# Moving VectorE work in a fused two-block kernel: rotation and conv taps behind the gated products, a residual sum one tile later, four taps ahead of a weight remainder

## The chip, the cores and the metric

The kernel runs on one core of a Trainium2 chip. Its time is device time in microseconds (us) for one launch. TensorE (PE in the profile) multiplies, VectorE (DVE) does elementwise work, ScalarE (ACT) applies functions and copies, SyncE (SP) issues weight loads and GpSimd (POOL) does a little elementwise work. Each engine works through its own list in order, and waits on counters that the others raise.

## The reference, cut to what matters

512 positions with 1024 channels pass through two blocks. The first has a conformer branch (a gated product, a causal depthwise convolution of 31 taps, layer norm), a state-space branch with a chunked scan ("the scan"), and a gated feed-forward. The second adds 16 meta positions (528 in all) and runs two layers, called layer 0 and layer 1. What the change touches:

```python
# block 1, conformer branch
v = a * sigmoid(g); v = causal_dwconv(v, dw_w, dw_b)          # 31 taps
# block 2, each layer l
a = rmsnorm(h, mix_pre_g[l]); proj = a @ w_in[l]
q = partial_rope(q, cos, sin); k = partial_rope(k, cos, sin)    # "rotation"
u = c_gate * hc; y = dwconv3(u, conv_w[l]); y_conv = b_gate * y # 3 taps on a gated product
y_attn = sliding_window_gqa_sinks(q, k, v, sinks[l])
h = h + rmsnorm(concat(norm(y_attn), norm(y_conv)) @ w_out[l], mix_post_g[l])
a = rmsnorm(h, mlp_pre_g[l])
h = h + rmsnorm(square(relu(a @ w_up[l])) @ w_down[l], mlp_post_g[l])
```

## The kernel before, in words

**Precision and weights.** Channels lie on the 128 partitions, positions on the free axis; there are eight channel tiles (0 to 7). Every product is made of three passes with fp32r parts: high input times high weight (line 635), low input times high weight (L637), high input times low weight (L639). The weights come as a stream of 1 MB units. SP loads a unit into `raw`, ScalarE copies it to `whi` (L1348, L1431), VectorE subtracts to get `wlo` (L2056, `low_at`, `low_next`), and TensorE then runs the unit. ScalarE's copy waits until TensorE has finished the unit that used the slot. All of it is double-buffered.

**The border of the two layers (lines 3009 to 3041).** The last two down-projection units of layer 0 are computed in two halves of 264 positions. `zadd(u, h)` (L3004) adds a half of such a unit to `zres`, after the unit is done; `zsquares` (L2222, through `add_square_half`) adds its square, made by ScalarE (L1436), into `acc2`. `residual_half(..., 0, ...)` (L2224 to L2247) runs for the first half over tiles k = 0 to 7: scale `zres` (L2239), add it to the residual `hres` (L2241), then `low_half(k - 1)` (L2233), which forms the low part `alo` of the tile before and waits for ScalarE's high part `ahi` of that tile (L1446). After that it runs what `beside` names for k. Before the change the work of the second half stands at k = 0 (`second`: sum and square of the last unit but one), k = 2 (`third`: sum of the last unit) and k = 3 (`fourth`: its square added). ScalarE's own list there is: square of the last unit, weight copy of layer 1's second unit (`split_unit`, L1431), `ahi` of tile 3, root of the second half (L1440), `ahi` of tiles 4 to 7. TensorE's list (`first_units`, L845) is: layer 1's first unit on tiles 0, 1, 2, then the matmul that sums the second half's squares (`sum_half`, L842, which waits for `fourth`), then tiles 3 to 7, then the second unit.

**Layer 1's input projection (lines 1131 to 1180 and 2765 to 2822).** Units 0 to 2 give q, k and v. During unit 3 TensorE multiplies q and k by a swap matrix (`swap`, L1152) and VectorE finishes each rotation (`rope(j)`, three operations, L2770 to L2773; j = 4 is the key). `c_gate(j)` (L2779) reads the first tile of unit 3 + j, `gated(j)` (L2785) reads the second, writes `upad` and frees the PSUM banks. The order on VectorE is `rope(2)`, `rope(3)`, `rope(4)`, `gated(0)`. TensorE, when unit 3 is done, transposes v (L1170), waits for the fourth rotation and v before that and for the fifth (`rope_ok` 5, L1172) after it, and starts unit 4, which also waits for the banks that `gated(0)` frees. The change does not touch TensorE's list.

**The attention steps (lines 2876 to 2912).** Ten steps n share units 4 to 8, a step being half a unit (u = 4 + n // 2, m = n % 2). On VectorE a step has a softmax (L2839 to L2850), a weight remainder, `output(n - 1)` (L2857 to L2863), `conv(u - 4)` when m = 0 (three taps and a scale, L2792 to L2797) and `c_gate` (m = 0) or `gated` (m = 1). TensorE turns the probabilities (L1198, waiting for the exponentials and for the output before last), makes scores (L1182), and runs half a unit around the outputs (L1208). In layer 1 the first block of queries is not needed, so the first step with scores is `n0` = 2, and `second` = 3.

**The long convolution beside `ssm_out` (lines 2573 to 2589).** For each of eight units VectorE adds taps (L2319) for the conformer's tiles, multiplies the unit's result by its gate (`gb`, L2581, after ScalarE's copy into `ring`) and forms the remainder of a coming weight unit. `late_tiles` is [4, 6], so `long_taps(late_tiles, w0, w0 + 2, ...)` is four operations.

Of the kernel before, what the change touches and what calls it, by code (L numbers as in the profile page):

```python
# [39 lines left out]
TAPS_GATE = 3  # L40
# [103 lines left out]
def build(nc, xT, metaT, wstream, cols_d, heads_d, const1_d, const2_d, acs_d, outT):  # L144
    ctx = ExitStack()
    with ctx:
# [214 lines left out]
        def early_scores(n0):  # L361

            return (n0, STEPS - 1) if n0 else (STEPS - 1,)
# [5 lines left out]
        def split2(ap):  # L369
            return ap.rearrange("p (a c) -> p a c", a=2)  # L370

        def col(name, k):
            a = COLS[name][0]
            if isinstance(k, int):
                return cols[:, a + k:a + k + 1]
            return cols[:, bass.ds(k + a, 1)]
# [9 lines left out]
        def cut(t, start, n):  # L386
            return t[:, start:start + n] if isinstance(start, int) else t[:, bass.ds(start, n)]
# [28 lines left out]
        def after(eng, counter, value):  # L416
            eng.wait_ge(counter.sem, value + counter.base)
# [1628 lines left out]
        def _(dve):  # L2046
# [15 lines left out]
            def low_next(stage, i, s):  # L2062

                u = 2 * i + (stage.u0 + s + 2)
                if not by_cast(u):
                    low(stage.slot(s), u, u if CAST0 < u <= CAST_END else None)
# [157 lines left out]
            def residual_half(n, g, span, h, hn, hg, beside):  # L2224

                after(dve, n["std"], h + 1)
                v.reciprocal(span.cols(rstd, h), span.cols(std, h))
                drain()

                def low_half(k):  # L2230
                    if hn is not None:
                        after(dve, hn["hi"], h * KD + k + 1)
                        v.scalar_tensor_tensor(span.half(alo, k, h), span.half(hres, k, h), col(hg, k),  # L2233
                                               span.half(ahi, k, h).bitcast(F32), ALU.mult, ALU.subtract
                                               ).then_inc(hn["lo"].sem, 1)

                for k in range(KD):
                    t, r = span.half(zres, k, h), span.half(hres, k, h)
                    v.scalar_tensor_tensor(t, t, col(g, k), span.cols(rstd, h), ALU.mult, ALU.mult)  # L2239
                    drain()  # L2240
                    v.tensor_tensor(r, r, t, ALU.add).then_inc(n["dve"].sem, 1)  # L2241
                    if k:
                        low_half(k - 1)
                    if k in beside:
                        beside[k]()
                low_half(KD - 1)
# [62 lines left out]
            def long_taps(tiles, a, b, start=None):  # L2309

                for w in range(a, b) if start is None else [start + k for k in range(a, b)]:
                    drain()  # L2312
                    for u in tiles:
                        src, acc = cut(vpad, u * VW + w, T), cut(vout, u * T, T)
                        wc = col("conv_w", u * TAPS + w)
                        if isinstance(w, int) and w == 0:
                            v.tensor_scalar(acc, src, wc, col("conv_b", u), ALU.mult, ALU.add)
                        else:
                            v.scalar_tensor_tensor(acc, src, wc, acc, ALU.mult, ALU.add)  # L2319
# [83 lines left out]
            late_tiles = [u for u in range(4, KD, 2)]  # L2403
# [166 lines left out]
            n = (TAPS - TAPS_GATE) // 4  # L2570
            assert 4 * n + TAPS_GATE == TAPS
            stage_s = WORK["ssm_out"]
            for i in range(0, KD // 2):
                for s in range(2):
                    w0, w1 = (n + 1) // 2 * s, n if s else (n + 1) // 2
                    if i + s == 0:
                        low_next(stage_s, 0, 0)
                    long_taps(late_tiles, w0, w0 + 2, n * i + TAPS_GATE)
                    hold(dve, ring_ok, 2 * i + (s + 1), "dve")
                    t = cut(gb, 2 * T * i + s * T, T)  # L2580
                    v.tensor_tensor(t, t, ring[s][:, :], ALU.mult).then_inc(ring_used, 1)  # L2581
                    if 2 * i + s + 1 < KD:
                        low_next(stage_s, i + s, 1 - s)
                    long_taps(late_tiles, w0 + 2, w1, n * i + TAPS_GATE)
                    w = LAST_TAPS + 2 * (2 * i + s)
                    long_taps([KD - 1], w, min(w + 2, TAPS))
                    w = 5 * (GROUPS - 1) + 2 * (2 * i + s)
                    long_taps([2], w, w + 2)
# [146 lines left out]
            for l, y in enumerate(layers):  # L2735
# [29 lines left out]
                def rope(j):  # L2765
                    after(dve, y["swap_ps"], j + 1)
                    raw_t = qraw[:, j * L:(j + 1) * L]
                    dst = qpad[:, j * QPAD + LEAD:(j + 1) * QPAD] if j < 4 else kpad[:, WIN + LEAD:KPAD]
                    drain()
                    v.tensor_tensor(split2(rot[:, 0:L]), split2(sin), wide(far + 2 * (j % 2)), ALU.mult)  # L2770
                    v.tensor_tensor(rot[:, L:2 * L], raw_t, cos, ALU.mult)
                    drain()
                    v.tensor_tensor(dst, rot[:, 0:L], rot[:, L:2 * L], ALU.add).then_inc(y["rope_ok"].sem, 1)  # L2773
# [7 lines left out]
                def gated(j):  # L2781

                    dve.wait_ge(unit_done, stage.u0 + 4 + j)
                    drain()
                    v.tensor_tensor(split2(upad[j % 2][:, 2:2 + L]), wide(near + 2), split2(cgate[j % 2][:, :]), ALU.mult  # L2785
                                    ).then_inc(psum_free[stage.slot((3 + j) % 2)], 1)

                def conv(j):

                    acc, up_ = yconv[:, j * L:(j + 1) * L], upad[j % 2]  # L2790
                    drain()
                    v.tensor_scalar(acc, up_[:, 0:L], col(w2, 3 * j), None, ALU.mult)  # L2792
                    for w in (1, 2):
                        drain()
                        v.scalar_tensor_tensor(acc, up_[:, w:w + L], col(w2, 3 * j + w), acc, ALU.mult, ALU.add)
                    drain()
                    v.tensor_tensor(acc, acc, rstd[:, :], ALU.mult)  # L2797
# [19 lines left out]
                c_gate(0)  # L2817
                rope(2)
                rope(3)
                rope(4)  # L2820
                gated(0)


                sinks = f"sinks_{l}"
# [52 lines left out]
                ahead, second = early_scores(n0), n0 + 1 if n0 else None  # L2877
                for n in range(STEPS):
                    u, m = 4 + n // 2, n % 2
                    if n >= n0 and n not in ahead and n != second:  # L2880
                        softmax(n)
                    if n == 0:
                        low_at(stage.u0 + 5)
                    elif m == 0:
                        low_at(stage.u0 + u + 1)
                    if n + 1 == second:
                        softmax(second)
                        output(n)
                    if n == 1:
                        conv(0)  # L2890
                    if n > n0 and n != second:
                        output(n - 1)
                    if n and m == 0 and u <= 7:
                        conv(u - 4)
                    if n >= n0 + 3 and m:
                        token_scale((n - 3) // 2)
                    if n + 1 == STEPS - 1:
                        softmax(n + 1)
                    if n == STEPS - 1:
                        add_square(y["n_conv"], 2)  # L2900
                    if u >= 7:
                        b_gate(2 * (u - 7) + m)
                    elif m == 0:
                        c_gate(u - 3)
                    else:
                        gated(u - 3)
                    if n0 and n + 1 == n0:
                        softmax(n0)
                    if n == STEPS - 2:
                        add_square(y["n_conv"], 0)  # L2910
                        add_square(y["n_conv"], 1)
# [102 lines left out]
                args = (y["n_mpost"], f"mlp_post_{l}", span)  # L3014
                folds = (nxt, f"mix_pre_{l + 1}")
# [15 lines left out]
                    zsquares(KD - 1, 1)  # L3031

                if nxt:
                    residual_half(*args, 0, *folds, {0: second, 2: third, 3: fourth})
                    low_at(after_.u0 + 1)
                    residual_half(*args, 1, *folds, {})
                else:
                    last_half(*args, 0, {0: second})
                    third()
                    fourth()  # L3040
                    last_half(*args, 1, {})
# [152 lines left out]
```

## Time and profile before

| | before |
|---|---|
| median of three runs | 2207.59 us (2207.06 to 2208.0) |
| profiled execution, its own time | 2209.11 us |
| span in the profile | 2207.3 us |
| TensorE busy | 2166.7 us, 98% |
| VectorE busy | 1419.1 us, 64% |
| ScalarE busy | 965.8 us, 44% |
| GpSimd busy | 59.0 us, 3% |
| DMA | mean 99 GB/s |

Busy TensorE is modelled from pipelined matmuls, so a successor starts before its predecessor's shown end. In a timeline row the first number is the start, the second the length, and a bracket says how long the engine had been idle and what ended that.

### The profile page before, as it was taken

The numbers are of one execution on the slowest core, as the hardware profiler recorded it, in microseconds if no ns is written. First come the engines' busy times: TensorE is split into PE (matmuls) and PEld (weight loads), VectorE is DVE, ScalarE is ACT, GpSimd is POOL, SyncE is SP. The second block draws the span as 40 slices with busy tenths as digits, with TensorE's granted clock in tenths as the row PEclk, the third lists the DMA queues.
The fourth block names the chain that finished last, engine by engine and source line by source line (L and its number), as shares of the span: only waits on it lengthen the run. The fifth ranks groups of instructions, "written<-read, shape, count | busy, mean of one in ns | idle before, by whom it ended". The sixth has DMA issues, their size and how long they took to land.

```text
span 2207.3 us, 31562 instructions
## 1 busy us (share of the span) xinstructions
PE 2166.7 (98%) x12892; PEld 1894.8 (86%) x12892; DVE 1419.1 (64%) x1830; ACT 965.8 (44%) x1401; POOL 59.0 (3%) x58
## 2 busy tenths in 40 slices
PE   9999999999999999999999999999999999999997
PEld 6887777788788888888999999999999989888887
DVE  4876898999868555645876784145367668622544
ACT  5447776632625444423457443133233664422321
POOL 1000111000000000000000000000000000000001
PEclk9999999999999999999999999999999999999999
DMA  4234556222222222243211222222222112222221
GB/s 155 96 110 130 155 160 159 90 96 96 86 103 80 96 96 96 97 153 134 100 58 58 77 83 91 96 91 82 96 77 100 58 60 94 96 96 96 95 96 58
DMA packets 36843, 217.63 MB, mean 99 GB/s; under 512 B 5056, under 2 KB 7104, under 8 KB 12128
## 3 DMA queue, kind: packets, MB, share of 16 engines
q1 hardware_dynamic: 27504, 182.99, 23.8%
q0 software_dynamic: 2880, 20.97, 4.0%
q10 hardware_dynamic: 6320, 11.70, 1.7%
q8 instruction: 101, 1.65, 0.3%
q14 instruction: 38, 0.31, 0.0%
HBM read 213.48 MB, written 2.16 MB: 98 GB/s over the span
## 4 chain that ended last, share of the span: by engine, by line
PE 77%; DVE 12%; ACT 3%; DVEq 3%; issue 2%; DMA 2%; ACTq 1%; POOL 0%; SPq 0%; POOLq 0%
PE PS L635 24%; PE PS L639 24%; PE PS L637 24%; DVE vout L2319 4%; DVE wlo L2056 2%; PE PS L1208 1%; DVEq L2312 1%; DMA wlo<-weights 1%; PE PS L1182 1%; PE PS L1198 1%; ACT m_slot L1606 1%; DVE acc L2211 0%; DVE hres L2241 0%; PE PS L1223 0%; ACTq L1608 0%
## 5 line engine op out<-in xcount | busy, mean ns | idle before, releaser
L639 PE MATMUL PS<-ahi,wlo 128*128 128x512 f32 (+2 forms) x2333 | 704.3, 337 | 0.0
L635 PE MATMUL PS<-ahi,whi 128*128 128x512 f32 (+2 forms) x2237 | 677.6, 340 | 7.4 <-DVE wlo L2056 2.2
L637 PE MATMUL PS<-alo,whi 128*128 128x512 f32 (+2 forms) x2237 | 667.3, 335 | 0.0
L2056 DVE TENSOR_TENSOR wlo<-raw,whi 128x2048 fp32r<-128x2048 f32 x160 | 366.3, 2290 | 427.6 <-ACT whi L1348 426.3
L1348 ACT ACTIVATE whi<-raw 128x2048 fp32r<-128x2048 f32 x156 | 298.8, 1916 | 634.4 <-PE PS L639 631.8
L639 PEld LDWEIGHTS PS<-ahi,wlo 128*128 128x128 f32 x2333 | 404.8, 188 | 46.9
L635 PEld LDWEIGHTS PS<-ahi,whi 128*128 128x128 f32 x2237 | 387.6, 188 | 64.7 <-issue 14.6
L637 PEld LDWEIGHTS PS<-alo,whi 128*128 128x128 f32 x2237 | 386.9, 188 | 42.8 <-issue 1.0
L635 PE MATMUL PS<-f2hi,whi 128*128 128x264 f32 (+2 forms) x800 | 214.9, 314 | 0.0
L637 PE MATMUL PS<-f2lo,whi 128*128 128x264 f32 (+2 forms) x800 | 214.9, 314 | 0.0
L639 PE MATMUL PS<-f2hi,wlo 128*128 128x264 f32 (+2 forms) x800 | 214.8, 314 | 0.0
L2319 DVE SCALAR_TENSOR_TENSOR vout<-vpad,cols,vout 128x512 f32<-128x512 f32 x240 | 178.5, 754 | 18.1 <-issue 1.9
L635 PEld LDWEIGHTS PS<-f2hi,whi 128*128 128x128 f32 x800 | 136.1, 188 | 8.7
L637 PEld LDWEIGHTS PS<-f2lo,whi 128*128 128x128 f32 x800 | 135.9, 188 | 8.9
L639 PEld LDWEIGHTS PS<-f2hi,wlo 128*128 128x128 f32 x800 | 135.8, 189 | 8.8
L1966 ACT ACTIVATE f2hi<-rl 128x528 fp32r<-128x528 f32 (+1 forms) x64 | 40.7, 639 | 112.5 <-DVE rl L2971 112.3
L635 PE MATMUL PS<-fhi,whi 128*128 128x512 f32 x176 | 69.0, 392 | 0.0
L639 PE MATMUL PS<-fhi,wlo 128*128 128x512 f32 x176 | 68.5, 389 | 0.0
L637 PE MATMUL PS<-flo,whi 128*128 128x512 f32 x176 | 68.5, 389 | 0.0
L2070 DVE SCALAR_TENSOR_TENSOR fg<-PS,cols,fg 128x511 f32<-128x511 f32 x88 | 63.8, 745 | 4.3 <-ACT fg L1750 1.0
L1821 ACT ACTIVATE sc<-sc,small 128x256 f32<-128x256 f32 (+1 forms) x72 | 34.9, 486 | 50.3 <-DVEq L2851 50.3
L2975 DVE TENSOR_TENSOR f2lo<-rl,f2hi 128x528 fp32r<-128x528 f32 (+1 forms) x64 | 44.4, 696 | 19.1 <-ACT f2hi L1966 16.2
(389 smaller groups left out, 2823.9 us busy)
## 6 DMA issues: line engine op xcount, KB each, us to landing
raw<-weights SPq DMA_DIRECT2D x169, 1024.0 KB, 4.8
wlo<-weights POOLq DMA_DIRECT2D x10, 1024.0 KB, 9.1
acs_b<-acs_rows ACTq DMA_DIRECT2D x20, 256.0 KB, 5.1
raw_hi<-weights POOLq DMA_DIRECT2D x5, 1024.0 KB, 5.6
whi<-weights POOLq DMA_DIRECT2D x5, 1024.0 KB, 10.3
const<-const ACTq DMA_DIRECT2D x2, 1232.0 KB, 5.3
x_in<-x_t SPq DMA_DIRECT2D x4, 512.0 KB, 6.0
out_t<-hres SPq DMA_DIRECT2D x16, 128.0 KB, 1.7
```

Source lines behind the costliest of these rows:

```text
L635: nc.tensor.matmul(o, wh, h, start=first, stop=False)
L637: nc.tensor.matmul(o, wh, h, start=False, stop=False)
L639: mm = nc.tensor.matmul(out[j], wl, hi[j], start=False, stop=last)
L1182: mm = nc.tensor.matmul(bank(far + z, 256 - k0, jj * 256 + k0), qpad[64 * z:64 * z + 64, j * QPAD + b * WIN:j * QPAD + (b + 1) * WIN], kpa ...
L1198: mm = nc.tensor.transpose(bank(far + 2 + kb, P, j * P), sc[n % 2][:, j * 256 + kb * P:j * 256 + (kb + 1) * P], ident)
L1348: nc.scalar.activation(whi[slot][:, :], raw[slot][:, :], ACT.Copy).then_inc(hi_ready, 1)
L1821: nc.scalar.activation(p, p, ACT.Exp, bias=small[:, 8 * z + j:8 * z + j + 1], accum_out=small[:, 16 + 8 * z + j:17 + 8 * z + j])
L1966: nc.scalar.activation(cut(f2hi, 4 * W * i + (2 * s + m) * W, W), rl[2 * s + m][:, 0:W], ACT.Copy).then_inc(f2hi_ok.sem, 1)
L2056: v.tensor_tensor(wlo[s][:, :], whole[:, :], high[:, :].bitcast(F32), ALU.subtract).then_inc(lo_ready, 1)
L2070: return v.scalar_tensor_tensor(acc[:, sh:n], ps[:, 0:n - sh], w, acc[:, sh:n], ALU.mult, ALU.add)
L2319: v.scalar_tensor_tensor(acc, src, wc, acc, ALU.mult, ALU.add)
L2975: v.tensor_tensor(cut(f2lo, c, W), rl[2 * s + m][:, 0:W], cut(f2hi, c, W).bitcast(F32), ALU.subtract).then_inc(f2lo_ok.sem, 1)
```

## The change

It moves VectorE instructions within VectorE's list in four places; no instruction is added or removed, and no other engine's list changes.

1. In the first pass of the loop beside `ssm_out`, four taps stand ahead of the weight remainder `low_next(stage_s, 0, 0)` instead of behind it.
2. In layer 1, `gated(0)` stands ahead of `rope(4)`; layer 0 keeps its order.
3. In layer 1's step 2, `conv(1)` leaves its place ahead of `c_gate(2)` and stands behind `gated(2)` in step 3. In layer 0 `second` is None and nothing changes.
4. At the border, `third` stands at tile 3 instead of 2 and `fourth` at tile 4 instead of 3.

```diff
@@ the loop beside ssm_out
+                    long_taps(late_tiles, w0, w0 + 2, n * i + TAPS_GATE)
                     if i + s == 0:
                         low_next(stage_s, 0, 0)
-                    long_taps(late_tiles, w0, w0 + 2, n * i + TAPS_GATE)
@@ each layer, before the steps
                 rope(2)
                 rope(3)
+                if l:
+                    gated(0)
                 rope(4)
-                gated(0)
+                if not l:
+                    gated(0)
@@ the steps
-                    if n and m == 0 and u <= 7:
+                    if n and m == 0 and u <= 7 and n + 1 != second:
                         conv(u - 4)
...
                         gated(u - 3)
+                    if n == second:
+                        conv(u - 4)
@@ the layers' border
-                    residual_half(*args, 0, *folds, {0: second, 2: third, 3: fourth})
+                    residual_half(*args, 0, *folds, {0: second, 3: third, 4: fourth})
```

## Rows read from the trace of the kernel before

**Rows 1.** Page, busy us (share of span) and instructions, each engine.
```profile
PE 2166.7 (98%) x12892; PEld 1894.8 (86%) x12892; DVE 1419.1 (64%) x1830; ACT 965.8 (44%) x1401; POOL 59.0 (3%) x58
```
**Rows 2.** Waits of TensorE from 1620 to 1700: total us, times, longest.
```profile
PE PS L635 <- DVE alo L2233: 2.0, 5, 0.6
```
**Rows 3.** Timeline of VectorE, the border: start us, length us, operation [idle before].
```profile
1635.12 0.43 DVE L3004 TENSOR_TENSOR zres<-zres,PS 128x264 f32<-128x264 f32 x1 [1.35 <-PE PS L639]
...
1636.61 0.49 DVE L2233 SCALAR_TENSOR_TENSOR alo<-hres,cols,ahi 128x264 fp32r<-128x264 f32 x1
1637.19 0.43 DVE L2222 TENSOR_TENSOR acc<-acc,sq 128x264 f32<-128x264 f32 x1
...
1638.45 0.49 DVE L2233 SCALAR_TENSOR_TENSOR alo<-hres,cols,ahi 128x264 fp32r<-128x264 f32 x1
...
1639.77 0.49 DVE L2233 SCALAR_TENSOR_TENSOR alo<-hres,cols,ahi 128x264 fp32r<-128x264 f32 x1
```
**Rows 4.** Timeline of ScalarE, the border.
```profile
1635.96 1.90 ACT L1431 ACTIVATE whi<-raw 128x2048 fp32r<-128x2048 f32 x1
1637.77 0.50 ACT L1446 ACTIVATE ahi<-hres,cols 128x264 fp32r<-128x264 f32 x1
1638.64 0.48 ACT L1440 ACTIVATE std<-PS,cols 128x264 f32<-128x264 f32 x1 [0.38 <-PE PS L842]
1639.02 0.51 ACT L1446 ACTIVATE ahi<-hres,cols 128x264 fp32r<-128x264 f32 x1
```
**Rows 5.** Timeline of TensorE, the border.
```profile
1637.15 0.39 PE L635 MATMUL PS<-ahi,whx 128*128 128x264 f32 x1 [0.62 <-DVE alo L2233]
...
1638.00 0.61 PE L842 MATMUL PS<-acc,const 128*128 128x264 f32 x2
...
1645.91 0.36 PE L635 MATMUL PS<-ahi,whi 128*128 128x264 f32 x1 [1.22 <-DVE wlo L2056]
```
**Rows 6.** Timeline of VectorE, layer 1's last rotation and first gated product.
```profile
1691.41 0.70 DVE L2770 TENSOR_TENSOR rot<-const,PS 128x528 f32<-128x528 f32 x1
...
1693.61 0.71 DVE L2785 TENSOR_TENSOR upad<-PS,cgate 128x528 f32<-128x528 f32 x1
```
**Rows 7.** Timeline of ScalarE there: the weight copy released by unit 3's end.
```profile
1693.30 1.92 ACT L1348 ACTIVATE whi<-raw 128x2048 fp32r<-128x2048 f32 x1 [13.88 <-PE PS L639]
```
**Rows 8.** Timeline of TensorE there: the start of unit 4.
```profile
1694.47 0.48 PE L635 MATMUL PS<-ahi,whi 128*128 128x264 f32 x2 [0.66 <-DVE upad L2785]
```
**Rows 9.** Timeline of VectorE, layer 1's steps 2 to 4.
```profile
1721.66 0.49 DVE L2792 TENSOR_SCALAR yconv<-upad,cols 128x528 f32<-128x528 f32 x1
...
1724.71 0.71 DVE L2779 TENSOR_TENSOR cgate<-PS,mu 128x528 f32<-128x528 f32 x1
...
1726.31 1.23 DVE L2839 SCALAR_TENSOR_TENSOR sc<-PS,const 128x1024 f32<-128x1024 f32 x1
...
1732.21 0.42 DVE L2863 TENSOR_TENSOR y_tok<-PS,small 128x256 f32<-128x256 f32 x1
```
**Rows 10.** Timeline of TensorE, the same steps.
```profile
1726.35 0.48 PE L635 MATMUL PS<-ahi,whi 128*128 128x264 f32 x2 [1.08 <-DVE upad L2785]
...
1734.06 1.04 PE L1198 MATMUL PS<-const,sc 128*128 128x128 f32 x8
```
**Rows 11.** Timeline of ScalarE, the copy released by unit 5's end.
```profile
1723.37 1.91 ACT L1348 ACTIVATE whi<-raw 128x2048 fp32r<-128x2048 f32 x1 [0.60 <-PE PS L639]
```
**Rows 12.** Timeline of VectorE, the first pass beside ssm_out.
```profile
470.05 2.29 DVE L2056 TENSOR_TENSOR wlo<-raw,whi 128x2048 fp32r<-128x2048 f32 x1 [2.84 <-ACT whi L1348]
472.43 2.90 DVE L2319 SCALAR_TENSOR_TENSOR vout<-vpad,cols,vout 128x512 f32<-128x512 f32 x4
...
476.18 2.29 DVE L2056 TENSOR_TENSOR wlo<-raw,whi 128x2048 fp32r<-128x2048 f32 x1 [0.24 <-ACT whi L1348]
```
**Rows 13.** Windows: stretch, length, PE, PEld, DVE, ACT, POOL busy, granted clock, DMA.
```profile
14.00:18.00 4.00, 4.00 (x40) 1.64 (x39) 2.19 (x4) 2.52 (x4) 2.37 (x1) 0.57 0.02 4
362.00:372.00 10.00, 7.72 (x42) 6.18 (x42) 9.33 (x18) 6.58 (x11) 0.65 (x1) 1.00 0.77 197
```

## The prediction

> **What bounds the kernel now.** I read the page first: TensorE is busy 2166.7 us of a span of 2207.3 us [rows 1], so only about 40 us are left in which it does nothing, and a reordering on VectorE can act only on those holes or make new ones. Next I asked for TensorE's waits by stretch, then for the timelines of the three engines at each of the four places. What the reader is to see: in the stretch of the border TensorE waits five times for VectorE's low parts, 2.0 us in all [rows 2], and once 1.22 us for a weight remainder [rows 5]; at layer 1's unit 4 it waits 0.66 us and at unit 6 1.08 us for a gated product [rows 8, 10]. These are the holes that the change aims at, 5 us together, or 0.22% of the time.
>
> **The border.** No part of the change adds or removes an instruction or a DMA; each moves some on VectorE, and what SP loads depends on them only through the weight remainders. Take times as before the change until something moves. VectorE waits 1.35 us ahead of `third` for the last unit's end, and `third` starts at 1635.12 [rows 3]. With tile 3's two operations and `alo` of tile 2 ahead of it, this hole is filled: `alo` of tile 2 starts earlier by the hole's 1.35 us and by the 0.58 us that a sum takes with its drain (1637.19 - 1636.61 [rows 3]), at 1634.7, and its 0.49 us end just as `third` may start. So TensorE runs tile 2 with no wait (0.62 us saved [rows 5]) and `third` starts at the same 1635.12. Then tile 4's two operations follow, in the place of tile 3's, to 1636.6. Next in VectorE's list is `alo` of tile 3, and it needs ScalarE's `ahi` of tile 3. ScalarE's list has the 1.90 us weight copy ahead of that, from 1635.96, released by the same unit's end; `ahi` of tile 3 runs from 1637.77 to 1638.27 [rows 4]. Before the change VectorE came for it at 1638.45, after `fourth`; now it comes 1.7 us too early and stands still with `fourth` queued behind it. `alo` of tile 3 starts at 1638.30, `fourth` 0.58 us later (1637.19 - 1636.61 [rows 3]) at 1638.88 and ends at 1639.31. TensorE took 0.85 us for tile 2 (1638.00 - 1637.15 [rows 5]), would be through it at about 1637.3, and waits for `fourth` ahead of L842. L842 moves from 1638.00 to about 1639.38, 1.38 later. ScalarE's root follows L842 by 0.64 us (1638.64 - 1638.00 [rows 4, 5]), so at 1640.02, and `ahi` of tile 4 comes 0.38 behind it at 1640.40 to 1640.91 [rows 4]. `alo` of tile 4 starts at 1640.95 instead of 1639.77 [rows 3]: 1.18 us late. From there the loop is VectorE's chain as before, tile by tile, then the weight remainder for the second unit, for which TensorE was already waiting (1.22 us [rows 5]); so the second unit starts 1.18 us later, at 1647.1, and VectorE and ScalarE are late by the same. Cost: +1.2 us. Bounds: if L842 followed `fourth` with no distance and the other distances shrank by a drain, +0.8; if TensorE is slower to pick up after a hole of 2 us, +1.6. A gain here would need `ahi` of tile 3 early: the hole of 1.35 us that is filled, less 0.04 us of rounding, -1.3. ScalarE's order is untouched, so I take +1.2.
>
> **The last rotation.** VectorE's three rotation operations start at 1691.41 and the gated product behind them at 1693.61 [rows 6], 2.20 us later, of which 0.09 is the drain that shows between any two dependent operations (470.05 + 2.29 to 472.43 [rows 12]). Unit 3 ends when ScalarE's copy is released, 1693.30 [rows 7], so the rotation lies wholly beside TensorE's unit 3: it costs nothing. With the product ahead of it, VectorE waits from 1691.4 to about 1693.38 with the rotation queued behind; the product takes its 0.71 us, to 1694.09, the rotation starts a drain later, at 1694.18, and ends 2.11 us on, at 1696.29. TensorE's unit 4 waits for both. Before, it started 0.15 us after the product's end (1693.61 + 0.71 to 1694.47 [rows 6, 8]); now the rotation is what comes last, and it starts at 1696.44. Cost: +1.97 us, the wait going from 0.66 to 2.63. Behind the rotation on VectorE stands a weight remainder for unit 5, and behind that the load on SP's queue that it releases; TensorE needs the first when unit 4 ends and the second a unit later. Bounds: the rotation's 2.20 us whole, and 1.8 if the product is released 0.2 us sooner than ScalarE's copy shows. A gain is excluded as long as L1172 stands: the later of the two can't come earlier in this order.
>
> **The conv taps.** `conv(1)` takes 3.05 us (1724.71 - 1721.66 [rows 9]). Without it `c_gate(2)` starts at 1721.66, `gated(2)` must wait for unit 5, whose end shows in ScalarE's release at 1723.37 [rows 11], and runs 1723.42 to 1724.13, while TensorE is still busy with turning and scores. The wait of 1.08 us ahead of unit 6 goes [rows 10]. Then `conv(1)` runs from 1724.22 to 1727.2 and the softmax of step 4 starts at 1727.27, where it started at 1726.31 [rows 9]: 0.96 later. Behind it in VectorE's list are a weight remainder and the output that TensorE needs before it turns the next probabilities. That output ends at 1732.63 + 0.96 = 1733.59 [rows 9]; TensorE would come for it at 1734.06 - 1.08 = 1732.98 [rows 10], and with 0.15 us of release it starts at 1733.74. So 0.76 of the 1.08 us is given back there, and 0.32 stays. ScalarE's next steps are 0.96 late as well and cost at most another 0.1 at the turn of the output tile. I take -0.3. Bounds: -1.1 if nothing is given back, +1.0 if the 0.96 us of delay passes to TensorE whole.
>
> **The four taps.** VectorE idles 2.84 us ahead of the remainder at 470.05; four taps take 2.90 and stood right behind it [rows 12]. They fit into the hole to within 0.1 us. But the next remainder, at 476.18, was waiting for ScalarE already (0.24 us [rows 12]), and ScalarE for TensorE. So the hole only moves behind the gate product, and everything from 476.18 on is as before. TensorE has no wait in this stage. 0.0 us; bounds -0.24 and +0.1.
>
> **The sum.** 1.2 + 1.97 - 0.3 + 0.0 = +2.9 us. The profiled execution took 2209.11 us for its span of 2207.3, 1.5 over the median of the runs; it would take 2212.0 and its span 2210.2. Against the median: 2207.59 + 2.9 = 2210.5 us, 0.13% more. About 0.2%, 4.4 us, is what a measurement of this kernel can tell from no change.
>
> **Rivals.** *A, the border is neutral or gains* (2208.6 us): if the wait for `ahi` of tile 3 costs VectorE only what the hole ahead of `third` gave, as two ends of one exchange, the border comes out between -1.3 and +0.6, say -0.7, and 1.97 - 0.3 - 0.7 = +1.0. For it: VectorE is what TensorE waits for here. Against: `fourth` lies behind the wait, and L842 and the root hang on `fourth`. *B, all holes close* (2205.0 us): the gated product, not the rotation, is what releases unit 4, so that its banks come 0.2 us sooner; the conv's whole 1.08 and the border's whole 1.3 are gained: -2.6, 0.12% faster. For it: each hole in the trace names exactly the operation that now comes earlier. Against: L1172, the 1.90 us copy [rows 4], and the output [rows 9]. *C, the clock falls* (2212.2 us or more, slower): TensorE now stands still for about 2.1 us at the border and 2.6 us ahead of unit 4. After a sparse stretch with short matmuls near the start the granted clock of 14 to 18 us is 0.57, so some 3.4 us of the 4 ran at the lower level of 1.2 GHz [rows 13]; where TensorE sets the pace, half of that, 1.7 us, is lost. One such fall gives 2.9 + 1.7 = +4.6, and two +6.3 (2213.9); the first already passes 4.4 us. Against: the stretch 362 to 372 has 2.28 us without TensorE work and a clock of 1.00 [rows 13], and the hole at unit 4 has dense work on both sides. The border is where it would decide, since TensorE would wait there ahead of nearly each tile.
>
> The Trainium skill, "TensorE: Matmul & The Clock Gate", Part 1, says that the clock drops to half after a stretch in which TensorE was idle and comes back only with sustained activity. By that rule a long enough hole would cost as in C; the trace agrees with a fall, and shows with the 2.28 us hole that one of this size alone need not bring it.
>
> **Chances.** Forecast 0.66; A 0.15; B 0.06; C 0.13. The forecast's own range, from its bounds, is 2208.9 to 2212.3. The range for 8 in 10 takes in most of A and the lower case of C: 2207.6 to 2212.4. Faster than 0.2% needs -4.4 us, which not even B gives: 0.02. Slower than 0.2% is C and the forecast's upper edge (rotation 2.2, border 1.6, conv +1.0): 0.13. The rest, 0.85, is within 0.2%.
>
> **What would show it.** In the changed kernel: VectorE's `alo` of tile 3 waits over 1 us for ScalarE's L1446, TensorE waits some 2 us ahead of L842, and the wait for the second unit's `wlo` stays near 1.2. Ahead of unit 4 of layer 1 TensorE waits 2.6 us and the releaser is `kpad` (L2773), not `upad`. The wait of 1.08 us for `upad` is gone and one of 0.6 to 0.8 us stands ahead of L1198, 8 us on. In the first pass beside `ssm_out` the idle of 2.8 us stands ahead of the second remainder instead of the first. I am wrong if unit 4 is released by `upad`, if L842 starts before 1638.5 relative to the same border, or if the granted clock falls in the windows behind either hole.

## The result, and the profile after

The changed kernel takes 2211.62 us in the median of 17 runs (2210.25 to 2216.32); the kernel before, run between them, 2208.32 (2206.6 to 2211.71). The ratio is 1.0020, with an interval of 1.0013 to 1.0026: slower by 2.9 to 5.7 us, clear of no change. The medians are 3.3 us apart and the means 3.8. With the later runs the means are 2212.6 (28 runs) and 2208.6 (118 runs of the kernel before): 4.0 us. The time lies in my range, and the sum's +2.9 us is near it, but I had given 0.85 to "within 0.2%", which I took for what can't be told from no change.

TensorE's waits after the change (waiting instruction, releaser, total us, times, longest), first from 1620 to 1700, the border and the rotation, then from 1730 to 1800, the steps:

```profile
PE PS L635 <- DVE kpad L2773: 2.5, 1, 2.5
PE PS L842 <- DVE acc L2222: 2.1, 1, 2.1
PE PS L635 <- DVE alo L2233: 0.8, 1, 0.8
PE PS L635 <- DVE wlo L2056: 0.8, 1, 0.8
PE PS L1152 <- DVE qpad L2773: 0.3, 1, 0.3
...
PE PS L1198 <- DVE y_tok L2866: 0.7, 1, 0.7
```

Both holes of the forecast are there: 2.1 us ahead of L842, where before L842 waited for nothing [rows 5], and 2.5 us ahead of unit 4 with `kpad` as releaser in place of 0.66 us with `upad` [rows 8]. The 1.08 us ahead of unit 6 [rows 10] are gone and 0.7 us ahead of L1198 have come.

VectorE at the border after the change, to be held against [rows 3]; this execution came to the border 1.31 us sooner, so `third` at 1633.81 answers to 1635.12:

```profile
1633.28 0.49 DVE L2233 SCALAR_TENSOR_TENSOR alo<-hres,cols,ahi 128x264 fp32r<-128x264 f32 x1
1633.81 0.43 DVE L3009 TENSOR_TENSOR zres<-zres,PS 128x264 f32<-128x264 f32 x1
...
1636.98 0.49 DVE L2233 SCALAR_TENSOR_TENSOR alo<-hres,cols,ahi 128x264 fp32r<-128x264 f32 x1 [1.61 <-ACT ahi L1446]
1637.57 0.43 DVE L2222 TENSOR_TENSOR acc<-acc,sq 128x264 f32<-128x264 f32 x1
...
1639.72 0.49 DVE L2233 SCALAR_TENSOR_TENSOR alo<-hres,cols,ahi 128x264 fp32r<-128x264 f32 x1 [0.81 <-ACT ahi L1446]
```

`third` no longer waits. `alo` of tile 3 waits 1.61 us for ScalarE's `ahi`, with the square's sum (L2222) queued behind it. ScalarE's and TensorE's side of the same stretch, with the copy of 1.90 us ahead of that `ahi`:

```profile
1634.65 1.90 ACT L1431 ACTIVATE whi<-raw 128x2048 fp32r<-128x2048 f32 x1
1636.46 0.49 ACT L1446 ACTIVATE ahi<-hres,cols 128x264 fp32r<-128x264 f32 x1
1638.81 0.48 ACT L1440 ACTIVATE std<-PS,cols 128x264 f32<-128x264 f32 x1 [1.86 <-PE PS L842]
```

```profile
1638.06 0.71 PE L842 MATMUL PS<-acc,const 128*128 128x264 f32 x2 [2.11 <-DVE acc L2222]
1640.27 0.39 PE L635 MATMUL PS<-ahi,whx 128*128 128x264 f32 x1 [0.78 <-DVE alo L2233]
1645.87 0.36 PE L635 MATMUL PS<-ahi,whi 128*128 128x264 f32 x1 [0.76 <-DVE wlo L2056]
```

VectorE at the rotation, against [rows 6]: it stands still 2.04 us for the gated product, then rotates. TensorE's unit 4 starts 0.05 us after `kpad` is done:

```profile
1693.27 0.71 DVE L2785 TENSOR_TENSOR upad<-PS,cgate 128x528 f32<-128x528 f32 x1 [2.04 <-PE PS L639]
1694.07 0.70 DVE L2770 TENSOR_TENSOR rot<-const,PS 128x528 f32<-128x528 f32 x1
...
1695.47 0.71 DVE L2773 TENSOR_TENSOR kpad<-rot 128x528 f32<-128x528 f32 x1
```

```profile
1696.23 0.51 PE L635 MATMUL PS<-ahi,whi 128*128 128x264 f32 x2 [2.52 <-DVE kpad L2773]
```

The four taps now fill ScalarE's 2.84 us [rows 12], and the hole has moved to the next remainder, as worked out; TensorE waits nowhere in that stage:

```profile
466.00 2.90 DVE L2319 SCALAR_TENSOR_TENSOR vout<-vpad,cols,vout 128x512 f32<-128x512 f32 x4
468.81 2.28 DVE L2056 TENSOR_TENSOR wlo<-raw,whi 128x2048 fp32r<-128x2048 f32 x1
...
474.86 2.29 DVE L2056 TENSOR_TENSOR wlo<-raw,whi 128x2048 fp32r<-128x2048 f32 x1 [3.16 <-ACT whi L1348]
```

What I had not priced, and had named as a sign that I am wrong, shows in a window behind the border's hole (PE, PEld, DVE, ACT, POOL busy, granted clock, DMA share, GB/s): the clock is 0.57.

```profile
1640.00:1644.00 4.00, 3.73 (x17) 3.54 (x18) 3.67 (x9) 2.13 (x4) 0.00 (x0) 0.57 0.01 2
```

**Stretches.** Whole spans differ by several us from one execution to the next before they even reach the border: the copy L1431 starts between 1632.5 and 1638.2 us in the 14 profiles, and of all edits only that of the taps stands ahead of it. So each edit is read between marks of its own profile. *Border*: from the start of that copy (just behind the last unit's end) to the second unit's first matmul. *Rotation*: from there to unit 4's first matmul. *Steps*: from there to the first matmul of the output projection (L646). What is left behind that is 414.7 to 414.9 us in all. The clock was looked through up to the last matmuls; the tail, in which TensorE is done, is left out of the column.

| kernel | border | rotation | steps | edits in it; where the clock fell (below 0.99 in a 4 us window) |
|---|---|---|---|---|
| before | 9.95 | 48.56 | 98.08 | none; start |
| changed | 11.22 | 50.36 | 98.02 | all; border |
| e1 | 11.22 | 48.52 | 98.00 | rotation undone; border |
| e2 | 9.94 | 50.40 | 97.96 | border undone; scan |
| e3 | 11.52 | 48.32 | 97.99 | late wait; border |
| e4 | 11.97 | 50.37 | 99.42 | border's hole filled; unit 4 |
| e5 | 9.53 | 50.41 | 99.33 | tile 3 early; scan, unit 4 |
| e6 | 9.79 | 50.40 | 98.02 | fourth first; start |
| e7 | 9.94 | 48.55 | 97.96 | conv alone; none |
| e8 | 8.63 | 48.26 | 99.11 | repaired; none |
| e9 | 11.31 | 50.40 | 98.04 | unit 4's hole filled; start, border |
| e10 | 8.63 | 48.30 | 96.99 | conv in step 5; start, scan |
| e11 | 11.23 | 50.42 | 99.52 | all again; start, border, unit 4 |
| e12 | 9.95 | 50.41 | 99.63 | rotation alone; unit 4 |

Against the kernel before, the change costs 1.27 at the border and 1.80 at the rotation and brings 0.06 in the steps: +3.0 us with an undisturbed clock.

### The profile page after: what moved, and what is told of

Same layout as the page of the kernel before. It is cut to its first block, busy times and chain, and to the rows that moved or that the text cites. A ratio compares the mean times of both kernels' runs of the same rounds, so it can differ in the third digit from the quotient of the medians.

```text
span 2209.0 us, 31562 instructions
## 1 busy us (share of the span) xinstructions
PE 2166.7 (98%) x12892; PEld 1896.6 (86%) x12892; DVE 1419.1 (64%) x1830; ACT 965.4 (44%) x1401; POOL 59.0 (3%) x58
## 4 chain that ended last, share of the span: by engine, by line
PE 79%; DVE 12%; ACT 3%; DVEq 3%; issue 2%; DMA 1%; ACTq 1%; POOL 0%; POOLq 0%
PE PS L635 25%; PE PS L639 24%; PE PS L637 24%; DVE vout L2319 4%; DVE wlo L2056 2%; PE PS L1208 1%; DVEq L2312 1%; DMA wlo<-weights 1%; PE PS L1182 1%; PE PS L1198 1%; ACT m_slot L1606 1%; DVE acc L2211 0%; DVE hres L2241 0%; PE PS L1223 0%; ACTq L1608 0%
## 5 line engine op out<-in xcount | busy, mean ns | idle before, releaser
L1348 ACT ACTIVATE whi<-raw 128x2048 fp32r<-128x2048 f32 x156 | 298.8, 1916 | 634.3 <-PE PS L639 631.7
```

The lines of the kernel that those rows point to most:

```text
L1348: nc.scalar.activation(whi[slot][:, :], raw[slot][:, :], ACT.Copy).then_inc(hi_ready, 1)
```

## The experiments

**e1, the rotation undone.** The second hunk of the change taken back.

> The change without its second edit (layer 1 rotates before the gated product again). My theory: the wait of TensorE ahead of unit 4 falls from 2.5 us (released by kpad, L2773) to 0.66 us (released by upad), and the kernel takes 1.85 us less than the changed one: about +1.0 us against the kernel before in the traces (border +1.27, conv -0.3). Rival, the clock: if the hole ahead of unit 4 also lets TensorE's clock fall in some executions, undoing it takes off more than 2 us on average and the spread of the times gets smaller. Rival, the rotation is hidden: less than 0.5 us.

Measured: 2209.4 us (median of 12), ratio 1.0006 (0.9997 to 1.0014). The wait ahead of unit 4 is 0.64 us again, the rotation's stretch 48.52: 1.84 us off, as expected. Its mean is 2209.8, 2.8 us below the changed kernel's, which leans to the clock's part; but the spread of its times is no smaller (6.7 us against 6.1), as that rival had wanted.

**e2, the border undone.** The last hunk taken back.

> The change without its fourth edit (third and fourth at tiles 2 and 3 again). My theory: no wait of 2.1 us ahead of L842, alo of tile 3 waits for nothing, and 1.2 us less than the changed kernel: about +1.6 us against the kernel before (rotation +1.85, conv -0.3). Rival, the clock: the granted clock of 0.57 that the changed kernel shows in the 4 us behind that hole is what makes its slow executions (2213 to 2216 us, clock 0.993 to 0.996); then this kernel has no such fall, its runs lie within 1.5 us of each other as those before, and its mean is over 2 us lower than that of the changed kernel.

Measured: 2210.88 us, ratio 1.0012 (1.0004 to 1.0021). The border's stretch is 9.94, 1.28 off. The mean is 2.5 us over that of the kernel before, where 1.6 was expected, and a run of 2216.54 is among the twelve, so the rival fell in that form: the border's hole is not what makes the slowest executions.

**e3, the wait put where the rotation is needed.**

```diff
-                after(pe, y["rope_ok"], 5)      # ahead of unit 4
...
+                    if n == n0:
+                        after(pe, y["rope_ok"], 5)   # ahead of the first scores
```

> The changed kernel, with TensorE's wait for the fifth rotation moved from ahead of unit 4 to ahead of the first scores (two half units later in layer 1). My theory: the order gated product before rotation costs only through this wait; now unit 4 starts 0.15 us after the gated product, the wait is about 0.4 us and is released by upad, and the kernel takes 2.0 us less than the changed one, 0.9 us over the kernel before. Rival: the gated product itself comes late for another reason (release of unit 3), then the wait stays above 1 us.

Measured: 2208.81 us, ratio 0.9995 (0.9986 to 1.0003). Unit 4 waits 0.41 us and is released by `upad`; the stretch is 48.32, 2.04 off and 0.24 under the kernel before. So the new order at the rotation is good in itself, and L1172 alone turns it into a loss. The whole time missed the expectation: the stretches of this profile add up to +1.2 us against the kernel before, +0.9 was expected, and the mean is 0.4 below it, with an interval that ends at +0.7. Why these runs were so fast is open.

```profile
1694.23 0.48 PE L635 MATMUL PS<-ahi,whi 128*128 128x264 f32 x2 [0.41 <-DVE upad L2786]
```

**e4, the border's hole filled.** `spin(14, ...)` ahead of `sum_half` in `first_units`.

> The changed kernel, with 14 small matmuls (128x128, into the bank of the sum that follows) ahead of L842 at the border, so that TensorE works through most of its hole of 2.1 us. If the fall of the clock behind the hole costs time: the granted clock at 1640 to 1644 is 1.00, the spread of the times narrows to that of the kernel before and the mean is over 1 us lower than that of the changed kernel. If the fall is hidden behind VectorE's chain, as I think of the profiled execution (TensorE waited for VectorE there in any case): the clock is 1.00, and the time is that of the changed kernel within 0.4 us, +2.8 us against the kernel before.

Measured: 2212.39 us, ratio 1.0017 (1.0009 to 1.0026). I had sized the filling wrong: 14 of them take 3.29 us, and L842 starts 1.34 us after the square's sum instead of 0.49. The border's stretch grows by 0.75, so a delay of L842 passes to the second unit nearly whole. The clock behind the border stays at 1.00. As a test of what the fall there costs it is spoiled by its own 0.75 us. It fell behind unit 4's hole instead, where TensorE has dense work:

```profile
1692.00:1696.00 4.00, 1.48 (x8) 1.24 (x7) 3.83 (x5) 3.79 (x4) 0.00 (x0) 0.84 0.02 4
1696.00:1700.00 4.00, 4.00 (x27) 4.00 (x26) 0.98 (x1) 0.00 (x0) 0.00 (x0) 0.73 0.42 135
```

```profile
1694.83 0.81 PE L635 MATMUL PS<-ahi,whi 128*128 128x264 f32 x2 [2.52 <-DVE kpad L2774]
1695.44 0.64 PE L637 MATMUL PS<-alo,whi 128*128 128x264 f32 x2
1695.88 0.64 PE L639 MATMUL PS<-ahi,wlo 128*128 128x264 f32 x2
1696.32 0.64 PE L635 MATMUL PS<-ahi,whi 128*128 128x264 f32 x2
```

The pairs start 0.44 us apart instead of 0.24 to 0.25, and the steps take 99.42 instead of 98.0 us.

**e5, tile 3 early.**

```diff
-                refold(0, (0, 1, 2))
+                refold(0, (0, 1, 2, 3))
...
-                refold(0, (3,))
```

> The changed kernel, with ScalarE's ahi of tile 3 taken ahead of the last unit's square and of the 1.90 us weight copy (one instruction moved on ScalarE). My theory: the new order at the border loses only because alo of tile 3 waits for that copy. Then the waits of 1.61 us ahead of alo 3 and of 2.1 us ahead of L842 shrink to under 0.5 us, the border turns from +1.27 to about -0.5 against the kernel before (the root of the second half still holds up ahi of tile 4), and the kernel is 1.8 us faster than the changed one, +1.0 against the kernel before. Rival: the loss comes from the place of the square's sum itself (fourth at tile 4); then L842 still waits over 1.5 us.

Measured: 2211.46 us, ratio 1.0010 (1.0001 to 1.0019), with two falls of the clock in its profile. The mean is 2.0 us over that of the kernel before, where 1.0 was expected. The wait ahead of L842 is 0.41 us, and the border's stretch 9.53: 1.69 under the changed kernel's and 0.42 under the kernel before.

```profile
1637.46 0.71 PE L842 MATMUL PS<-acc,const 128*128 128x264 f32 x2 [0.41 <-DVE acc L2221]
```

**e6, fourth first.** `{0: second, 3: lambda: (third(), fourth())}`.

> The changed kernel, with fourth run right behind third at tile 3, ahead of the alo of tile 3 that waits for ScalarE. My theory: the wait of alo 3 stays (about 1 us), but L842 no longer hangs on it and waits under 0.5 us, the root of the second half comes as soon as ScalarE is through its copy, and the border costs between -0.2 and 0 against the kernel before: 1.3 us faster than the changed one, +1.4 against the kernel before. Rival, that the wait of alo 3 is what costs and not what is queued behind it: then the kernel stays within 0.4 us of the changed one.

Measured: 2211.12 us, ratio 1.0009 (1.0000 to 1.0019). The border's stretch is 9.79, 1.43 under the changed kernel's, though `alo` of tile 3 still waits 0.80 us. The mean is 2.9 us over that of the kernel before, where 1.4 was expected. With e5 this settles the border: what costs is that the square's sum stands behind an operation that ScalarE's copy holds up.

```profile
1638.22 0.43 DVE L2222 TENSOR_TENSOR acc<-acc,sq 128x264 f32<-128x264 f32 x1 [0.60 <-ACT sq L1436]
1640.36 0.49 DVE L2233 SCALAR_TENSOR_TENSOR alo<-hres,cols,ahi 128x264 fp32r<-128x264 f32 x1 [0.80 <-ACT ahi L1446]
```

**e7, the conv alone.** The third edit on the kernel before.

> The kernel before with the third edit alone (conv(1) behind gated(2)). My theory: the wait of 1.08 us ahead of unit 6 goes and one of 0.68 to 0.8 us ahead of L1198 comes, so the kernel is 0.3 us faster than before, which the times can't tell from nothing. Rival, the whole 1.08 us is gained: no wait ahead of L1198. Rival, slower: a wait ahead of L1198 of over 1.1 us.

Measured: 2208.24 us, ratio 0.9998 (0.9989 to 1.0007). The 0.68 us ahead of L1198 is there, and the steps take 97.96 instead of 98.08: 0.1 us gained, not 0.3.

**e8, repaired.** The kernel before with the border's new order, ScalarE's `refold(0, (0, 1, 2, 3))` early and `refold(0, (4, 5))` ahead of the root, the rotation's new order with e3's wait, `conv(1)` taken out of step 2, and in step 4

```diff
                     if n > n0 and n != second:
                         output(n - 1)
+                    if second and n == second + 1:
+                        conv(1)
```

> All the ideas of the change with what stood in their way moved too: third and fourth at tiles 3 and 4 with ScalarE's ahi of tile 3 ahead of its weight copy and those of tiles 4 and 5 ahead of the root; the gated product ahead of the last rotation with TensorE's wait for the rotation ahead of the first scores; conv(1) behind output(3) of step 4, where it delays neither the softmax nor the output. The taps of the first edit stay as before. My theory: border -1.3, rotation -0.2, conv -1.0, together -2.5 us against the kernel before (0.9989), and no hole of TensorE over 1.3 us between 1620 and 1760. Rival: VectorE is short of time in the steps and conv(1) comes back as a wait further on; then the gain is 1.5 us or less.

Measured: 2207.92 us, ratio 0.9997 (0.9988 to 1.0006). Border 8.63 (-1.32) and rotation 48.26 (-0.30) as expected. In the steps the rival won: TensorE waits 1.89 us for the diagonal, which is now behind two convs (`conv(1)` and `conv(2)`), and they take 99.11, 1.0 us more.

```profile
1740.14 1.16 PE L1224 MATMUL PS<-diag,y_tok 128*128 128x128 f32 x8 [1.89 <-DVE diag L2878]
```

**e9, unit 4's hole filled.** `spin(9, near)` ahead of the wait for `rope_ok` 5 in layer 1.

> The changed kernel, with nine small matmuls (0.235 us each in e4, 2.1 us together) in TensorE's hole of 2.52 us ahead of unit 4. So far the 4 us behind this hole show a fallen clock in e4 and e5 and not in the changed kernel's profile, e2 and e6; where it fell, the stretch from unit 4 to the turn in step 5 took 40.7 us instead of 39.3. If the hole's length is what lets the clock fall: no fall at 1692 to 1700, that stretch 39.3 us, the stretch before it 50.4 us as in the changed kernel, and a mean some 0.5 us under that of the changed kernel run beside it. If the falls there are chance: as often as before, and no difference of the means.

Measured: 2211.31 us, ratio 1.0014 (1.0005 to 1.0023). No fall there, steps 98.04, rotation 50.40, and a mean of 2210.9 against 2212.9 for e11 beside it, with a highest time of 2212.49 against 2216.74. The direction is that of the first theory; 2.0 us is more than the 0.5 expected, and part of it is chance (e11's slowest executions).

**e10, the conv in step 5.** As e8, with

```diff
                         token_scale((n - 3) // 2)
+                    if second and n == second + 2:
+                        conv(1)
```

> As e8 at the border and at the rotation, but conv(1) stands in step 5 behind token_scale, where VectorE stood idle for 3.0 us ahead of gated(3), instead of behind output(3), where it made TensorE wait 1.89 us for the diagonal. My theory: border -1.3, rotation -0.25, conv -1.1 with nothing given back: -2.7 us against the kernel before, no wait of TensorE over 0.5 us between unit 4 and the last step. Rival: the 3.05 us of conv(1) are as long as the idle time, gated(3) comes late and TensorE waits ahead of unit 7; then the conv's gain is 0.5 us or less.

Measured: 2205.47 us, ratio 0.9991 (0.9982 to 1.0000), 2.4 us below the kernel before in the median, 2.3 in the mean, though the interval just reaches no change. Its stretches are -1.32, -0.26 and -1.09, together -2.67. The conv stands where VectorE had been idle, and the gated product follows without a wait:

```profile
1741.48 0.50 DVE L2793 TENSOR_SCALAR yconv<-upad,cols 128x528 f32<-128x528 f32 x1
1742.05 1.61 DVE L2796 SCALAR_TENSOR_TENSOR yconv<-upad,cols,yconv 128x528 f32<-128x528 f32 x2
1743.74 0.71 DVE L2798 TENSOR_TENSOR yconv<-yconv,rstd 128x528 f32<-128x528 f32 x1
1744.53 0.71 DVE L2786 TENSOR_TENSOR upad<-PS,cgate 128x528 f32<-128x528 f32 x1
```

**e11, the change again.**

> The changed kernel once more, beside the others on one chip. By the stretches of the traces (border +1.27, rotation +1.82, conv -0.1) it takes 3.0 us more than the kernel before wherever the clock does not fall, and 1.4 us more again in those executions in which it falls behind the hole ahead of unit 4. So the mean lies 3.0 to 4.0 us over that of the kernel before, and the fastest runs of both 3.0 us apart. If the clock has no part in it, both differences are 3.0.

Measured: 2212.56 us (2210.82 to 2216.74), ratio 1.0020 (1.0011 to 1.0029). The mean is 4.8 us over that of the kernel before beside it, where 3.0 to 4.0 was expected, and the fastest run of each (2210.82, 2205.98) 4.8 apart, where 3.0 was expected; over all runs the fastest are 4.3 apart (2210.25, 2205.98), with 28 of the changed kernel against 118. So both expectations were missed; that the spread ahead of the border did it is likely, but not shown. Its profile has the fall behind unit 4's hole and steps of 99.52.

**e12, the rotation alone.**

> The kernel before with the second edit alone. My theory: the stretch from the second unit to unit 4 takes 50.4 instead of 48.56 us, nothing else changes, and the fastest runs are 1.8 us over those of the kernel before; the mean 1.8 to 2.4 over, as the clock falls behind the hole in a third of the executions or so. Rival, the delay is taken up later by a wait that gets shorter: under 1.0 us.

Measured: 2211.21 us, ratio 1.0011 (1.0002 to 1.0020), the mean 2.8 us over the kernel before, the fastest run 2.3. The stretch is 50.41 (+1.85); nothing takes it up later. The profile has the fall, and the steps take 99.63, 1.55 more than before:

```profile
1692.00:1696.00 4.00, 1.73 (x15) 1.49 (x13) 2.54 (x4) 2.76 (x2) 0.00 (x0) 1.00 0.00 0
1696.00:1700.00 4.00, 3.75 (x18) 3.75 (x19) 2.40 (x2) 1.23 (x3) 0.00 (x0) 0.57 0.14 25
1700.00:1704.00 4.00, 4.00 (x35) 4.00 (x35) 0.01 (x1) 0.00 (x0) 0.00 (x0) 1.00 0.61 242
```

## Why the prediction was half right

**The border, +1.2: right.** 1.27. The chain was the one forecast: `alo` of tile 3 waits 1.61 us (forecast 1.7), L842 2.11 us (2.1), and L842 starts 1.37 us later behind the copy's start (1.38); e5 and e6 show both links of it.

**The rotation, +1.97: right, a tenth too large.** 1.80 to 1.85. The gated product and the three operations behind it took 2.91 us, as forecast. But TensorE's first pass followed the end of `kpad` by 0.05 us, where I had taken over the 0.15 us behind the gated product; the rest is a product that started up to 0.07 us sooner than forecast. e3 shows that the wait at L1172 is the whole of it, which also rules out rival B here.

**The conv, -0.3: right in kind, too large.** -0.06 to -0.12. The wait ahead of L1198 came (0.68 us), and in e7 L1198 starts 0.30 us sooner behind unit 4's start, as forecast; of that 0.2 is lost behind it, where I had put "at most another 0.1".

**The taps, 0: right.** From the scan's L987 to the second remainder it is 109.68 us before the change and 109.66 after, and TensorE waits nowhere in that stage. No run has this edit alone; the two traces show it.

**The step that failed: the sum, which set the clock at nothing, and the 4.4 us that I took for the least that can be told from no change.** The sum kept the clock's fall as rival C with a chance of 0.13, as if all executions would do the one or all the other. The runs show a cost that comes in a part of the executions. The hole of 2.52 us ahead of unit 4 is in seven profiles (changed, e2, e4, e5, e6, e11, e12); in four of them the clock falls behind it, and the steps take 1.3 to 1.6 us more. In the other seven, e9 with the filled hole among them, it falls there in none. Four of seven times 1.45 is 0.8 us; with 3.0 from the stretches that makes 3.8, beside 4.0 measured between the means. The times of the other runs can be held against this: take from each kernel's mean, less that of the kernel before beside it, the sum of its stretches at an undisturbed clock. In the seven kernels with the hole 0.8 us is left on average (-0.3 to 1.7), in the six without it -0.4 (-1.7 to 0.4). So kernels with the hole do take more than their stretches. How much is uncertain, for single kernels scatter by a us or more, and how often the clock falls in unprofiled executions is not known: 0.8 us stays an estimate.

The second half of the step is the limit. 17 runs of each give an interval of 1.4 us to either side, so a change of 3 us can be told from nothing. Even the sum's own +2.9 should have been called slower, and most of the 0.85 on "within 0.2%" was misplaced. The range's upper bound was 0.2 us short as well: 1.6 + 2.2 + 1.0 + 0.1 is +4.9, so 2212.5 and not 2212.3.

My ground against rival C was a single hole in the scan with a clock of 1.00 [rows 13]. That hole is TensorE's wait ahead of L987, 2.25 us in that execution, and it is not the same in each: it is 0.39 to 3.40 us long in the 14 profiles. The clock falls behind it in three of them, at 2.88 (e2), 3.36 (e10) and 3.40 us (e5), and not at 2.94 (e12) and 2.96 us (e1), nor in the nine with 2.37 us or less. Two nearly equal holes, first e2's, then e12's:

```profile
365.80 1.75 PE L987 MATMUL PS<-const,c_slot 128*128 128x128 f32 x8 [2.88 <-DVE xdt L2421]
364.00:368.00 4.00, 2.17 (x12) 1.99 (x13) 3.76 (x9) 1.71 (x4) 0.00 (x0) 0.80 0.60 121
```

```profile
366.39 1.29 PE L987 MATMUL PS<-const,c_slot 128*128 128x128 f32 x8 [2.94 <-DVE xdt L2421]
364.00:368.00 4.00, 1.58 (x13) 1.40 (x14) 3.76 (x8) 2.11 (x3) 0.00 (x0) 1.00 0.70 143
```

So one row could not show that a hole of this kind leaves the clock alone, and the row was of a shorter hole than the forecast 2.6 us; I read it as though it settled the matter.

At the border the hole ahead of L842 is in five profiles (changed, e1, e3, e9, e11), with a fallen clock behind it in all five; in the other nine, where L842 waits 0.42 us at most, the clock does not fall there. It costs 0.0 to 0.3 us (11.22, 11.22, 11.52, 11.31, 11.23), because TensorE waits for VectorE there in most places: in the changed kernel slow passes eat the wait for `wlo` (0.76 for 1.22 us). What it costs is L842 itself, on which ScalarE's root hangs: the root starts 0.75 us behind L842 in three of the five, as in e5 at a clock of 1.00, but 0.83 in e9 and 1.05 in e3. So rival C's mechanism was right and its place was wrong: I looked for it at the sparse border, and it costs at the dense unit 4.

The Trainium skill, "TensorE: Matmul & The Clock Gate", Part 1, says that how many matmuls run at the lower level before the clock rises differs between runs of one kernel. The traces agree near the kernel's start, where the lower level lasts from nothing to some 12 us; that the fall itself comes in 4 of 7 executions is what the profiles of this case show.

## What to carry to other kernels

Before an operation is moved ahead on an in-order engine, look for what is queued behind it and whose list holds its input: here one copy of 1.90 us on ScalarE and one wait on TensorE turned two good orders into losses of 1.3 and 1.8 us, and moving those two with them, and `conv(1)` to step 5, gave 2.4 us below the kernel before. Put work that nobody waits for where its engine is already idle (conv(1) in step 5: -1.09 us), not merely behind the next urgent operation (step 4: +1.03). Price a hole of the sizes seen here (2.1 us and more) on TensorE with its length and with the clock's fall times its frequency over several profiles, and look at what follows: here the fall cost 1.3 to 1.6 us ahead of dense work and 0.0 to 0.3 where TensorE waited for VectorE anyway. Before one row is taken as proof, look whether the same place is the same length in another execution.

## What the runs showed of the hardware that I had not expected

One and the same hole lowers the granted clock in some executions and not in others: 4 of 7 at 2.52 us with dense work on both sides (between unit 3's last pass and unit 4's first, 3.1 us, stand only the five transposes of L1170), 5 of 5 at 2.11 us at the sparse border. In the scan, where the hole's length varies, it fell in 3 of the 5 profiles with 2.88 us or more and in none of the nine with 2.37 us or less. At unit 4 six to eight pairs of passes then started 0.44 us apart instead of 0.25, and the steps took 1.3 to 1.6 us more.

The same happens near the start of the kernel, for between 0 and some 12 us (windows 16 to 28 at 0.50 in e6, 0.50 to 0.51 in e11). ScalarE's first weight copy behind it (L1348) starts at 34.0 to 34.8 us in the nine profiles without a fall there, at 35.5 in the two with the short one (before, e9), at 36.5 in e10 and at 38.4 and 38.6 in e11 and e6: up to some 4 us. The border's start, 1632.5 to 1638.2 us, follows these two: without a fall at the start it is 1632.1 to 1633.0 us and the length of the scan's hole, and with one it is 1 to 4 us more. Those 5.7 us are of the size of the spread of one kernel's times (2206.0 to 2213.4 for the kernel before), and why stretches within a profile told more than spans. Why the scan's hole differs from one execution to the next is open.
